# Sums of squares as quarters of partitions, two pairs of FFN tiles opened side by side, and eight low weight parts on GpSimd

## The reference

```python
gate = jax.nn.sigmoid(rms_norm(h, g_ple[i]) @ w_ple_gate[i] + b_ple_gate[i])
h = h + gate * (p[i] @ w_ple_proj[i])
...
h = rms_norm_2(hs, norm_mix_pre[layer])
mix = pool_mixer(h, pool_w[layer], pool_scale[layer])
hs = hs + rms_norm_2(mix, norm_mix_post[layer])
h = rms_norm_2(hs, norm_ffn_pre[layer])
hs = hs + rms_norm_2(swiglu(h, w_gate_up[layer], w_down[layer]), norm_ffn_post[layer])
...
def pool_mixer(h, w_groups, scale):
    # per group of channels: mean over a trailing window of 2, 4, 8 or 16 tokens, minus the token,
    # then a product with w_groups[gi] and a factor scale
def rms_norm_2(x, g):
    y = xf * lax.rsqrt(jnp.mean(xf * xf, axis=-1, keepdims=True) + EPS)
```

## Time and profile before

| | us |
|---|---|
| median of 3 runs (lowest, highest) | 2164.06 (2163.53, 2164.28) |
| the profiled execution | 2166.01 |
| its span | 2164.20 |
| TensorE busy | 1950.9 (90%) |
| VectorE busy | 959.5 (44%) |
| ScalarE busy | 651.6 (30%) |
| GpSimd busy | 209.9 (10%) |

### The profile page before, as it was taken

The page is one execution under the profiler, slowest core; times in us unless marked ns, Lnnn a source line. Parts: engine busy times, 40 slices in busy tenths (PEclk is TensorE's granted clock), DMA queues, the critical chain, the costliest instruction groups (busy, mean ns, idle before and its releaser), DMA issues.

```text
span 2164.2 us, 32679 instructions
## 1 busy us (share of the span) xinstructions
PE 1950.9 (90%) x14022; PEld 1669.3 (77%) x14022; DVE 959.5 (44%) x1701; ACT 651.6 (30%) x1217; POOL 209.9 (10%) x284
## 2 busy tenths in 40 slices
PE   6887999949999999988799999997987969999997
PEld 4755788836666655668799999997855869999996
DVE  4744334352333223346653322347655584422456
ACT  5333323120110100135332222234445543222232
POOL 0022000000000000004210000003122230000012
PEclk9998999969999999999779999998999979999998
DMA  4211234549999999962011332333301224232242
GB/s 152 77 50 49 91 121 145 196 170 379 426 426 427 425 427 427 427 247 88 11 59 59 98 98 79 98 108 117 100 28 59 88 79 141 94 108 88 89 143 82
DMA packets 58085, 355.75 MB, mean 164 GB/s; under 512 B 6304, under 2 KB 8992, under 8 KB 45648
## 3 DMA queue, kind: packets, MB, share of 16 engines
q1 hardware_dynamic: 53968, 340.02, 41.7%
q0 software_dynamic: 3504, 12.73, 1.6%
q10 hardware_dynamic: 464, 0.85, 0.1%
HBM read 349.38 MB, written 4.19 MB: 163 GB/s over the span
## 4 chain that ended last, share of the span: by engine, by line
PE 71%; DMA 10%; DVE 10%; ACT 4%; POOL 3%; issue 2%; SPq 0%; ACTq 0%; POOLq 0%; DVEq 0%
PE bank L425 51%; DMA e<-in_we 8%; PE bank L610 7%; PE bank L632 4%; PE bank L782 1%; ACT SS L2308 1%; PE bank L471 1%; DVE ztmp L1590 1%; PE bank L643 1%; PE bank L644 1%; DVE scr L1241 1%; DMA B<-in_rel 1%; DVE SS L1734 1%; DVE wlo L1078 1%; POOL zacc L2413 1%
## 5 line engine op out<-in xcount | busy, mean ns | idle before, releaser
L425 PE MATMUL bank<-nhi,whi 128*128 128x256 f32 (+2 forms) x1504 | 439.1, 292 | 9.3 <-DVE nlo L1600 5.5
L425 PE MATMUL bank<-nhi,wlo 128*128 128x256 f32 (+2 forms) x1504 | 433.2, 288 | 0.0
L425 PE MATMUL bank<-nlo,whi 128*128 128x256 f32 (+2 forms) x1504 | 433.0, 288 | 0.0
L1078 DVE TENSOR_TENSOR wlo<-raw,whi 128x1024 fp32r<-128x1024 f32 x247 | 308.8, 1256 | 143.3 <-ACT whi L1848 139.5
L425 PEld LDWEIGHTS bank<-nhi,whi 128*128 128x128 f32 x1504 | 289.8, 193 | 13.9 <-issue 6.3
L1848 ACT CAST whi<-raw 128x1024 fp32r<-128x1024 f32 x247 | 257.0, 1043 | 123.1 <-PE bank L425 102.1
L425 PEld LDWEIGHTS bank<-nlo,whi 128*128 128x128 f32 x1504 | 289.4, 192 | 1.0
L425 PEld LDWEIGHTS bank<-nhi,wlo 128*128 128x128 f32 x1504 | 288.9, 192 | 1.5
L610 PE MATMUL bank<-e,xT 128*64 128x256 f32 x2048 | 237.0, 385 | 1.0 <-DVE xT L1370 1.0
L610 PEld LDWEIGHTS bank<-e,xT 128*64 128x64 f32 x2048 | 143.2, 138 | 82.7 <-issue 16.5
L425 PE MATMUL bank<-ghi,whi 128*128 128x256 f32 (+1 forms) x704 | 201.0, 286 | 0.0
(11 more groups left out here) (302 smaller groups left out, 2978.3 us busy)
## 6 DMA issues: line engine op xcount, KB each, us to landing
e<-in_we SPq DMA_DIRECT2D x96, 2048.0 KB, 34.5
raw<-in_w_down SPq DMA_DIRECT2D x64, 512.0 KB, 3.5
raw<-in_w_gate SPq DMA_DIRECT2D x48, 512.0 KB, 3.4
raw<-in_w_up SPq DMA_DIRECT2D x48, 512.0 KB, 3.5
raw<-in_w_q SPq DMA_DIRECT2D x12, 512.0 KB, 4.4
B<-in_rel POOLq DMA_DIRECT2D x8, 512.0 KB, 4.2
raw<-in_w_gc SPq DMA_DIRECT2D x8, 512.0 KB, 3.8
raw<-in_w_ga SPq DMA_DIRECT2D x8, 512.0 KB, 4.4
```

The costliest lines, as they stand in the source:

```text
L425: i = e.matmul(o, a, x[:, k0 + k, c0:c1], start=(k == 0 and n == 0), stop=(k == j.K - 1 and n == 2))
L1078: e.tensor_tensor(wlo[wslot(u)][:], raw[u % NRAW][:], whi[wslot(u)][:].bitcast(F32), ALU.subtract).then_inc(*hit("dve_low", ("lo", u)))
```

## The change

**Sums of squares.** All eight norms (`ple`, `pre0`, `mp0`, `fp0`, two ranges each) go by `square_sum` now. It is turned round: 32 columns of ones are stationary, and a quarter of the tokens (64 or 68 columns of squares) moves; the four quarters q go to the partitions 32q to 32q + 31 of one bank. So the sums of the tokens lie along the free axis, four quarters on four groups of partitions. The root is taken in this form on 128 partitions x 64 or 68 columns (`rr`), and `spread` is four matmuls, each with one column of the identity, broadcast to 128 columns, as the stationary operand. There are no diagonals.

**Who takes the root.** `root_now` on VectorE, mean and root in eleven operations, for seven of the eight; `pre0` 1 keeps ScalarE's mean and GpSimd's root. Banks 6 and 7 hold sums and spreads (`SUMS`), so that `REST` is (4, 5) and the tiles of the opening use six banks.

**Opening.** `open_pairs` runs the first two pairs of tiles side by side: per chunk k the four tiles `fg` 0, `fu` 0, `fg` 1, `fu` 1 have three matmuls each, and the square sum of the chunk before follows. The last pair of pool products of range 1 stands in it at k = 4. The other two pairs follow as tiles. VectorE and ScalarE have an order of their own for this (`dve_open`, `act_open`).

**GpSimd.** The low parts of the eight units from `U_FFN` on are subtracted on GpSimd (`LO_POOL`), two of them before the root of `pre0` 1 and six behind it. It has no sums for these norms and no diagonals any more.

**Smaller ones.** The window of two tokens is one subtraction, with its half put into `pool_scale`. `mixed_post(0)` stands ahead of the windows of range 1.

The core of the diff:

```diff
-        REST = (4, 5, 6)
+        REST = (4, 5)
...
         def pe_pool():
-            for k in range(5, 8):
-                square_sum("pre0", 1, k)
-            pool_products(1, range(4), DENSE)
+            for n in range(2):
+                pool_products(1, (2 * n, 2 * n + 1), DENSE)
+                square_sum("mp0", 0, 2 * n)
+                square_sum("mp0", 0, 2 * n + 1)
+                square_sum("pre0", 1, 5 + n)
+            square_sum("pre0", 1, 7)
             pool_products(1, (4, 5), REST)
+            for k in range(4, 8):
+                square_sum("mp0", 0, k)
             spread("pre0", 1)
+            spread("mp0", 0)
+
+        def open_pairs(r, ps):
+            jobs = [(J[n, 0, i, r], (n, 0, i, r)) for i in ps for n in ("fg", "fu")]
+            outs = [take((*key, r), OPEN)[:, 0:RG[r][1] - RG[r][0]] for _, key in jobs]
...
             for k in range(8):
-                square_sum("mp0", 0, k)
-            pool_products(1, (6, 7), DENSE)
-            spread("mp0", 0)
+                if r == 0 and k == 4:
+                    pool_products(1, (6, 7), REST)
+                w.wait_ge(*at("n", "fp0", r, k))
+                for (j, key), o in zip(jobs, outs):
...
+                    for n, (a, x) in enumerate(((wh, nhi), (wh, nlo), (wl, nhi))):
+                        p = e.matmul(o, a, x[:, k, c0:c1], start=(k == 0 and n == 0), stop=(k == 7 and n == 2))
...
+                if k >= 1:
+                    square_sum("fp0", r, k - 1)
+            square_sum("fp0", r, 7)
...
         def square_sum(nm, r, k):
...
-            chunks = [(x, c) for x, c in CH[r].items() if c >= c0]
-            for x, c in chunks:
-                n = MT if x == 0 and k else 128
-                p = e.matmul(b[0:n, x:x + 1], sq[:, c - c0:c - c0 + n], ones[:, 0:1], start=(k == 0 and x == chunks[0][0]),
-                             stop=(k == 7 and x == chunks[-1][0]))
+            n = quarter(nm, r)
+            for q in range(4):
+                p = e.matmul(b[32 * q:32 * q + 32, 0:n], ones[:, 0:32], sq[:, q * n:(q + 1) * n], start=(k == 0),
+                             stop=(k == 7))
...
         def spread(nm, r):
...
+                for q in range(4):
+                    p = e.matmul(b[:, q * n:(q + 1) * n], ident[:, 32 * q:32 * q + 1].to_broadcast([128, 128]),
+                                 rr[:, r, 0, 0:n], start=True, stop=True)
...
-    SUMMED = [("ple", 0), ("pre0", 1)] + [(n, r) for n in ("mp0", "fp0") for r in range(2)]
+    SUMMED = [(n, r) for n in ("ple", "pre0", "mp0", "fp0") for r in range(2)]
...
+    LO_POOL = range(U_FFN, U_FFN + 8)
...
+        def root_now(nm, r):
+            n = quarter(nm, r)
+            y, xm, u = (rr[:, r, i, 0:n] for i in range(3))
+            w.wait_ge(*at("col", nm, r))
+            e.tensor_scalar(xm, bk("col", nm, r, n=n), 1.0 / D, EPS, ALU.mult, ALU.add).then_inc(
+                *hit("dve_mean", ("mean", nm, r), ("free", "col", nm, r)))
+            root(e, w, y, xm, u, "dve_root", nm, r)
...
+        def dve_open():
+            feed(U_FFN + 7)
+            mixed_post(0)
+            windows(1, 0)
+            windows(1, 1)
+            windows(1, 2)
+            scaled_products(1, 3)
+            root_now("fp0", 0)
+            windows(1, 3)
+            gate_now(0, 0)
+            gate_now(1, 0)
+            root_now("mp0", 1)
...
+        for u in LO_POOL:
+            if u == U_FFN + 2:
+                root_of("pre0", 1)
+            w.wait_ge(*at("hi", u))
+            e.tensor_tensor(wlo[wslot(u)][:], raw[u % NRAW][:], whi[wslot(u)][:].bitcast(F32), ALU.subtract).then_inc(
+                *hit("pool_low", ("lo", u)))
```

More of the change, by code:

```diff
@@ L726, in nothing @@
                 yield
-        def spread_in(n, nm, r):
-            yield from nothing(n)
-            spread(nm, r)
-            yield
-        REST = (4, 5, 6)
+        REST = (4, 5)
         def pool_products(r, ms, pool):
@@ L771, in square_sum @@
+        SUMS = {("ple", 0): 7, ("ple", 1): 6, ("pre0", 0): 7, ("pre0", 1): 6, ("mp0", 0): 7, ("fp0", 0): 6, ("mp0", 1): 7,
+                ("fp0", 1): 6}
         def square_sum(nm, r, k):
-            c0 = RNG[nm][r][0]
             if k == 0:
-                take(("col", nm, r), (7,))
+                take(("col", nm, r), (SUMS[nm, r],))
             b = bank[BANK["col", nm, r]]
@@ L793, in columns @@
             c0 = RNG[nm][r][0]
-            b = take(("col", nm, r), (7,) if nm in ("ple", "pre0") else SIDE)
+            b = take(("col", nm, r), SIDE)
             w.wait_ge(*at("acc", nm, r, 6))
@@ L806, in spread @@
             m0 = max(n0, 1)
-            b = take(("rb", nm, r), REST if nm in ("ple", "pre0", "mp0", "fp0") else SIDE)
+            if (nm, r) in SUMMED:
+                b = take(("rb", nm, r), (SUMS[nm, r],))
+                n = quarter(nm, r)
+                w.wait_ge(*at("root", nm, r))
+                for q in range(4):
+                    p = e.matmul(b[:, q * n:(q + 1) * n], ident[:, 32 * q:32 * q + 1].to_broadcast([128, 128]),
+                                 rr[:, r, 0, 0:n], start=True, stop=True)
+                p.then_inc(*hit("pe_norm", ("spread", nm, r)))
+                return
+            b = take(("rb", nm, r), SIDE)
             o = MT if n0 == 0 else 0
@@ L1449, in dve_ple @@
                     feed(U_FFN + (j - 12) // 3)
+                if j == 1:
+                    root_now("ple", 0)
                 for k in ((0, 1, 2), (3, 4), (5, 6, 7))[j] if j < 3 else ():
                     low(1, k)
+                if j == 11:
+                    root_now("pre0", 0)
                 if j >= 3:
@@ L1454, in dve_ple @@
                         gate_step(i)
+                if j == 6:
+                    root_now("ple", 1)
                 if j >= 13:
                     scaled_products(0, j - 13)
-                if j in (13, 14):
                     windows(0, j - 13)
@@ L1548, in dve_pool, with gate_now @@
         def dve_pool():
-            for g in range(4):
+            root_now("mp0", 0)
+            for g in range(3):
                 scaled_products(1, g)
+        def gate_now(i, r):
+            x0, x1 = RG[r]
+            w.wait_ge(*at("free", "rb", "fp0", r))
+            w.wait_ge(*at("out", "fg", 0, i, r))
+            if i >= 2 or r:
+                w.wait_ge(*at("g", 0, i - 2 if i >= 2 else i + 2, r if i >= 2 else 0))
+            e.tensor_tensor(sl[i % 2][:, x0:x1], bk("fg", 0, i, r, r, n=x1 - x0), rb[:, x0:x1], ALU.mult).then_inc(
+                *hit("dve_out", ("free", "fg", 0, i, r, r), ("gated", 0, i, r)))
```

270 lines of the change are left out of this document (168 added, 102 removed).

## The result

The changed kernel took 2135.44 us (median of 4 runs, 2134.59 to 2139.64) against 2164.17 before (4 runs): a ratio of 0.9871, 95% interval 0.9854 to 0.9888, so 28.7 us or 1.3% faster. The forecast was 2131.0 with a range of 2116 to 2150. The profiled execution took 2134.85, its span 2133.0.

What follows compares the result with a forecast made beforehand. The bound was the stretch 983 to 1163 (180.0 us, TensorE busy 155.4): dense 98.8, sums 22.4, spreads 5.4, idle 10.5, low clock 5.0, contention and handovers 4.9 make 147.0. That is 33.0 less: 2131.0 median, range 2116 to 2150.

Steps and rivals of the forecast that it cites:

- Sums of squares: 56 sums behind the first spread, each four matmuls at 0.40 us: 22.4 us, bounds 14.0 and 38.1.
- the rule at 2137: TensorE drains when tiling mode changes; by this rule 56 sums would cost some 6 us more, giving 2137.
- The 21.5 us of the dense work: Dense products between 983 and 1163: 120.3 us against 98.8 at full clock, the difference put down to the low clock.
- Spreads: Each spread becomes four matmuls with a stationary block 128 wide: 0.68 us taken, eight are 5.4.
- Roots: Root on VectorE 2.9 us, no diagonals; pre0 1 stays on GpSimd at 5.6 to 7.1; stretch idle 10.5 instead of 24.6.
- Low weight parts: Eight subtractions go from VectorE to GpSimd at 2.4 to 3 us; doubled VectorE operations delay first group 2.5, last windows 1.5.
- The opening: Paired tiles: first group starts at 1059.2 instead of 1081.5; TensorE sets the pace, waiting for VectorE only at the first chunk.
- The clock: The 7.3 us gap drops it to 1.2 GHz; two groups in range 0, one in range 1 and some tiles slow: 5 us.
- Rival (a): Clock stays low through the open groups: 2147, or 2158 with both ranges wholly low; chance 0.14.
- Rival (b): Sums are cheap (0.25 us each, -8.4) and contention is small (-3): 2120; chance 0.11.
- Rival (c): Sums at 0.68 us (+15.7), or GpSimd pulls VectorE's chain to 2.8 per chunk (+7): 2138 to 2147; chance 0.13.
- Rivals (d) and (e): (d) Sums at 2.3 us make it slower, 2237; (e) late opening cancels the gain, within 0.2% of 2164; chance 0.03 each.

Runs made afterwards that it cites:

- e7: The kernel of e1 with the root of mp0 0 on GpSimd (mean on ScalarE) behind that of pre0 1: 2134.38 us.
- e1: The changed kernel with the eight low weight parts subtracted on VectorE again instead of GpSimd: 2128.83 us, ratio to before 0.9832.
- e4: The changed kernel with the first four tiles of each range opened one after another, sums after each chunk of the first tile: 2139.3 us.

## Why the prediction was right, point by point

The time lay in the range, 4.4 us above the forecast, and the stretch gave 29.0 of the 33.0 forecast. Behind that stand terms that missed in both directions, so that the sum came so near is in part luck. By the three parts of the result, the forecast had 16.5 us from dense work, 7.3 from sums and spreads and 9.2 from idle time, contention and handovers; they gave 8.1, 16.0 and 4.9. By its own terms, with prices from the rows after: dense at the full clock 98.8 (forecast 98.8), sums 18.3 (22.4), spreads 7.6 (5.4), idle 150.4 - 130.7 = 19.7 (10.5, and 4.9 for contention and handovers). Of the 150.4 that leaves 6.0 for the low clock (5.0), and the rows show 5.6 of it: 3.6 on dense records and 2.0 on the two spreads in the gap.

**What bounds the kernel, and dense work.** Right: the whole gain lies between the ple stage and the first joint tile, and what follows still runs without a pause at 1.00.

**Sums of squares.** The term was 56 x 0.40 = 22.4. As measured, a block of adjacent sums costs 0.34 and each sum in it 0.12; 34 blocks and 56 sums are 11.6 + 6.7 = 18.3. So the term was 4 us too high, and its mechanism was wrong: I took the price as moving columns and put the switches beside it as a surplus. It is the other way round, most of the price comes once per block. The sentence that priced the rule at 2137 added the switches to a price of columns that was not there; that 2137 is nearer to the time measured than 2131.0 is luck.

**The 21.5 us of the dense work.** All of the 120.3 - 98.8 = 21.5 us was put down to the low clock, and this reading was wrong. After the change the dense lines are busy for 111.7, 12.9 above the 98.8, although the low clock accounts for only 3.6 there: the rest is in records beside a sum or a spread, which are longer (0.39 instead of 0.28 for the first). So part of the 21.5 was the price of stepping between kinds of matmul, which stays. (The row has 821 records, not 822, and the parts named add up to 819; that changes nothing.)

**Spreads.** 0.68 each was too low: 0.84 to 1.08 in the chain, so 2 us more in all.

**Roots.** 2.9 on VectorE was right where nothing disturbs it: mean and ten steps took 2.8 (1015.8 to 1018.6). The one on the path to the opening, of `mp0` 0, took 7.3 (1049.0 to 1056.4), 4.1 of it blocked. That VectorE's root is worth having on this path is shown by e7 (3.5).

**Low weight parts: the step that failed.** 2.5 and 1.5 us were counted for contention, as a doubling of short operations. It was 12.5 us on VectorE, 8.2 of them ahead of the first open group, and 2.2 more in the ple stage; taking it away gave 6.3 back (e1). The row that I used looks like a doubling where both engines' instructions are equally short. Together with two casts of ScalarE ahead of the first `nhi` (2.0) and the dearer spreads (1.95 each at the low clock), this set the first group back: forecast at 1059.2, less the 4.2 by which the whole execution was early, 1055.0; measured 1065.6.

**The opening.** From the first group to the joint tiles the forecast had 1129.7 - 1059.2 = 70.5, and it took 1129.5 - 1065.6 = 63.9. Of these 6.6 us, 24 sums in 16 blocks are 8.3 instead of 9.6, and range 1 began at the full clock, about 1. The rest is contention and handovers that I had put behind the first group and that fell ahead of it; no run splits it further. TensorE set the pace in the groups, as forecast, with one sum a group.

**The clock.** Right in its course in range 0: low in the gap and in two groups, high from the third on. In range 1 no group was slow, where one was forecast. Rival (a) did not come about; e4, with short groups and waits between them, had it in range 1. Rival (b) had the sums half right and the contention wrong. Rival (c) was wrong on the sums; contention was dear, as it said, but as whole blocked operations ahead of the opening and not as 2.8 per chunk, and TensorE did not wait once per chunk. What was too high and what was too low in the sum cancelled in part. Rivals (d) and (e) did not come about.

## What to carry to other kernels

Work moved from VectorE to GpSimd is not off VectorE when its operands are in SBUF: here an instruction of GpSimd held up a VectorE operation with two SBUF inputs until it ended (2.0 to 2.2 of 2.4). So price it by the length of GpSimd's instruction, and if it must be there, cut it short. The quarter-column matmuls between dense ones cost 0.34 per block and 0.03 per matmul, so put such matmuls in few blocks. And give TensorE enough to do at the pace of the engine that feeds it: groups of three matmuls fell to half clock when waits stood between them, and held the full clock for four turns when none did. Where one engine bounds the way, as VectorE does here, faster TensorE and better order elsewhere come out as waits. How the 28.7 us divide among turned sums, VectorE's roots and the paired opening is shown only in part: e4 and e7 price two of them, and no run changes the sums alone.

## What was not expected of the hardware

- A GpSimd subtraction of 128x1024 (2.38) lengthened one VectorE operation with two SBUF inputs by 2.0 to 2.2; cut into four parts of 0.7 to 0.9, it lengthened several by 0.4 to 0.5 each.
- GpSimd's root of 68 columns took 4.8 with VectorE idle or on products that read PSUM, and 8.0 beside its windows and subtractions.
- Four matmuls with 32 stationary columns each, on four quarters of the array, added 0.12 together; going over to them and back cost 0.34.
- Matmuls of ones by the identity in a gap raised the clock from 0.50 to 1.00 before the dense work came.
